# Preparing q, k and v between the input units, and running half of the attention heads inside the last seven of them

## The reference, cut to what matters

```python
h = rms_norm(x, g_mix)                                   # 1024 tokens x 1024
q_down, kv_down, k_rope, conv_in, gate_logits = split(h @ w_in)
q  = rms_norm(q_down) @ w_uq;   kv = rms_norm(kv_down) @ w_ukv      # 8 heads
k_nope, v = split(kv);          k = concat(k_nope, k_rope)
q, k = rope(rms_norm(q)), rope(rms_norm(k))              # norm per head, 96 wide
y_a = softmax(q @ k.T * scale, chunk-causal mask) @ v @ w_o
u = c_val * sigmoid(c_gate)
u = silu(layer_norm(causal_depthwise_conv(u, 31 taps) + b_dw))
y_b = u @ w_conv_out
x = x + (sigmoid(gA) * y_a + sigmoid(gB) * y_b) @ w_out
x = x + moe(rms_norm(x))                                 # 4 groups x 8 experts, top 2
```

## Time and profile before

| | us |
|---|---|
| median of 3 runs | 1285.98 (1282.86 to 1286.04) |
| the profiled execution, its own time | 1280.47 |
| its span, first to last instruction | 1278.4 |
| PE busy in the span | 1178.3 (92%) |
| DVE, ACT, POOL busy | 751.0 (59%), 469.2 (37%), 198.9 (16%) |
| mean granted clock of PE | 0.955 |
| PE busy and granted clock from 60 to 350 us (input units) | 288.93 of 290, 1.00 |
| from 350 to 460 us (attention, tiles 0 to 3) | 92.04 of 110, 0.88 |
| from 460 to 620 us (attention, tiles 4 to 7) | 153.48 of 160, 0.97 |
| from 620 to 710 us (branches) | 89.31 of 90, 0.98 |

### The profile page before, as it was taken

The page is one execution under the profiler, slowest core; times in us unless marked ns, Lnnn a source line. Parts: engine busy times, 40 slices in busy tenths (PEclk is TensorE's granted clock), DMA queues, the critical chain, the costliest instruction groups (busy, mean ns, idle before and its releaser), DMA issues.

```text
span 1278.4 us, 14988 instructions
## 1 busy us (share of the span) xinstructions
PE 1178.3 (92%) x5452; PEld 896.4 (70%) x5452; DVE 751.0 (59%) x992; ACT 469.2 (37%) x635; POOL 198.9 (16%) x243
## 2 busy tenths in 40 slices
PE   5999999999968999999899899849999988989996
PEld 5988888887645667767788788746676665666664
DVE  3338999993424455444466434476776656656663
ACT  4432111113443444444232211124555544554552
POOL 4010000000142232220000000011222321222211
PEclk8999999999969999999799999958999999999999
DMA  6011111110100000001330233495999999999980
GB/s 224 1 50 50 49 49 49 49 49 17 42 0 1 1 1 1 1 1 34 131 83 17 90 113 129 169 320 179 324 339 320 304 322 316 334 333 314 308 267 8
DMA packets 101542, 172.28 MB, mean 135 GB/s; under 512 B 11727, under 2 KB 45690, under 8 KB 101498
## 3 DMA queue, kind: packets, MB, share of 16 engines
q1 hardware_dynamic: 91002, 154.86, 35.8%
q0 software_dynamic: 10432, 16.81, 5.4%
q10 hardware_dynamic: 64, 0.02, 0.0%
HBM read 165.35 MB, written 27.26 MB: 151 GB/s over the span
## 4 chain that ended last, share of the span: by engine, by line
PE 71%; DMA 12%; ACT 4%; DVE 4%; issue 4%; POOL 2%; SPq 2%; DVEq 0%; ACTq 0%; POOLq 0%
PE pb L1224 15%; PE pb L1226 15%; PE pb L1225 15%; DMA wgu_raw<-in_w_e_up 11%; PE pb L1506 7%; PE pb L1364 4%; PE pb L1341 4%; PE pb L1353 2%; PE pb L1273 2%; PE pb L1478 2%; PE pb L1283 1%; PE pb L1424 1%; ACT wgu_hi L772 1%; SPq L414 1%; SPq L418 1%
## 5 line engine op out<-in xcount | busy, mean ns | idle before, releaser
L1165 DVE TENSOR_TENSOR wgu_lo<-wgu_raw,wgu_hi 128x2048 fp32r<-128x2048 f32 x72 | 164.7, 2289 | 89.3 <-ACT wgu_hi L772 87.8
L1506 PE MATMUL pb<-wed,midT 128*128 128x512 f32 x288 | 136.5, 618 | 23.1 <-DVE midT L1200 23.0
L873 DVE SCALAR_TENSOR_TENSOR cv<-up,dwc,cv 128x1024 f32<-128x1024 f32 x120 | 154.1, 1284 | 3.7
L1224 PE MATMUL pb<-hT_hi,ws_hi 128*128 128x512 f32 x384 | 151.7, 395 | 0.0
L772 ACT ACTIVATE wgu_hi<-wgu_raw 128x2048 fp32r<-128x2048 f32 x72 | 137.1, 1909 | 38.0 <-DMA wgu_raw<-in_w_e_up 33.8
L1226 PE MATMUL pb<-hT_hi,ws_lo 128*128 128x512 f32 x384 | 149.5, 389 | 0.0
L1225 PE MATMUL pb<-hT_lo,ws_hi 128*128 128x512 f32 x384 | 149.5, 389 | 0.0
L1224 PE MATMUL pb<-wgu_hi,hgT_hi 128*128 128x512 f32 x288 | 130.0, 452 | 0.0
L1506 PEld LDWEIGHTS pb<-wed,midT 128*128 128x128 f32 x288 | 54.6, 196 | 87.2 <-issue 62.5
L1226 PE MATMUL pb<-wgu_hi,hgT_lo 128*128 128x512 f32 x288 | 113.2, 393 | 0.0
L1225 PE MATMUL pb<-wgu_lo,hgT_hi 128*128 128x512 f32 x288 | 112.5, 391 | 0.0
(11 more groups left out here) (281 smaller groups left out, 2019.9 us busy)
## 6 DMA issues: line engine op xcount, KB each, us to landing
wgu_raw<-in_w_e_gate SPq DMA_DIRECT2D x36, 1024.0 KB
wgu_raw<-in_w_e_up SPq DMA_DIRECT2D x36, 1024.0 KB
wed<-in_w_e_down SPq DMA_DIRECT2D x36, 1024.0 KB, 16.3
ws_raw<-in_w_in SPq DMA_DIRECT2D x24, 512.0 KB, 3.9
xs<-in_x SPq DMA_DIRECT2D x8, 512.0 KB, 8.4
wout<-in_w_out SPq DMA_DIRECT2D x1, 4096.0 KB, 12.9
xb<-in_x SPq DMA_DIRECT2D x8, 512.0 KB, 5.2
h_rows<-h SPq DMA_DIRECT2D x8, 512.0 KB, 2.7
```

Source lines behind the costliest of these rows:

```text
L873: i = v.scalar_tensor_tensor(out=cv[:, c, :], in0=src, scalar=w, in1=cv[:, c, :], op0=ALU.mult, op1=ALU.add)
L1165: v.tensor_tensor(wgu_lo[q % SLOTS][:, :, ks, :], wgu_raw[q % SLOTS][:, :, ks, :], wgu_hi[q % 2][:, :, ks, :].bitcast(F32), ALU.subtract). ...
L1224: t_.matmul(out, w(0), m(0), start=start, stop=False)
L1506: m = t_.matmul(pb[:, 4 + h, :], midT[:, f, :], wed[q][:, f, h * 512:(h + 1) * 512], start=(f == 0), stop=(f == 1))
```

## The change

- **Preparation** (`prep`, the nine pieces of a tile in the order `PREP`) moves between the k-slices of the input units: 16 steps to a unit, tile t in units 1+2t and 2+2t, at the steps of `PREP_STEP`. Two PSUM banks (6 and 7) take turns. ACT copies `qdT` and writes the squares back into PSUM; DVE sums them `SUMS_LATE` = 4 steps and scales kT `K_LATE` = 2 steps after PE's step. The finished q, k, v of a tile go to DRAM and are loaded back later, as the space in SBUF is taken.
- **Heads 0 to 31** (tiles 0 to 3) run between the k-slices from unit 17, step 8, one head to three steps: `probs_T(n)` and `scores(n+2)` at one step, `pv(n)` two steps later. Tiles 4 to 7 follow the units as before, without preparation between the heads.
- **The gates** go to DRAM from a buffer of two (`gst`) and come back after attention, 16 transfers of 512 KB.
- **Taps**: 6 to a unit in place of 7, spread over the steps of a unit.
- **Layer norm** moves to tiles 4 to 6: POOL adds the four channel groups (six additions of 1024 columns), PE does four matmuls in place of 16, ACT and DVE do their parts between heads (`MEAN_AT` to `CONV_SPLIT`).
- **The split of the attention output** is made per tile from PSUM (`attn_hi`, `attn_lo`), `attn_T` of tiles 0 to 3 in heads 33 to 36, of tile 7 inside the first branch unit.

```diff
-TAPS_PER_UNIT = 7
+TAPS_PER_UNIT = 6
+STEPS = 2 * KD
+MIXED = 4 * 8
...
+        PREP = ("qdT", "q0", "q1", "kv0", "kv1", "qT0", "qT1", "kT0", "kT1")
+        PREP_STEP = (0, 3, 6, 9, 12, 22, 24, 28, 30)
+        PREP_UNIT = 1
+        SUMS_LATE, K_LATE = 4, 2
...
+        HEAD0, PER_HEAD = STEPS * 17 + 8, 3
+        attn_T_at = {MIXED + 1: 0, MIXED + 2: 1, MIXED + 3: 2, MIXED + 4: 3, 42: 4, 50: 5, 58: 6}
+        MEAN_AT, SQUARE_AT, VAR_AT, SQRT_AT = (37, 38), (39, 40), (44, 45), 46
+        RECIP_AT, SCALE_AT, SILU_AT, CONV_SPLIT = (47, 48, 49, 50), (51, 52), 53, (55, 56)
+        def prep_slot(kind, t):
+            n = len(PREP) * t + PREP.index(kind)
+            return n % 2, n // 2 + 1
...
+            sp.wait_ge(pv_ok, NTILE * HEADS)
+            for b in range(2):
+                sp.wait_ge(gate_out[b], 16 * GATE_UNITS // 2)
+            load_gates(0)
+            load_gates(1)
+            sp.wait_ge(cv_lo, NC)
+            sp.dma_start(wout[:, :, :], w_out[0].rearrange("(k p) c -> p k c", p=P)).then_inc(wout_in, 16)
...
@@ ACT: the loop over the input units
                 if u + 2 < IN_UNITS:
                     unit_hi(u + 2)
+                for s in range(STEPS):
+                    g = STEPS * (u + 1) + s
+                    if g in prep_at:
+                        prep(*prep_at[g])
+                    if g - 2 in scores_at:
+                        exps(scores_at[g - 2])
...
@@ DVE: before the loop over the input units
+            rotary_angles()
+            link(v.tensor_scalar(ss3[:, 2, :], ss3[:, 2, :], 1.0 / QK, EPS, ALU.mult, ALU.add))
@@ DVE: the loop over the input units
                 if u + 2 < IN_UNITS:
                     unit_lo(u + 2)
+                fresh = max(0, target - taps_done)
+                for s in range(STEPS):
+                    for k in range(taps_done + fresh * s // STEPS, taps_done + fresh * (s + 1) // STEPS):
+                        tap(k)
+                    g = STEPS * (u + 1) + s
+                    if prep_at.get(g - SUMS_LATE, ("",))[0] in ("q0", "q1", "kv0", "kv1"):
+                        prep(*prep_at[g - SUMS_LATE])
+                    if prep_at.get(g - K_LATE, ("",))[0] in ("kT0", "kT1"):
+                        prep(*prep_at[g - K_LATE])
+                    if g - 1 in probs_at:
+                        probs_out(probs_at[g - 1])
+                    if g - 1 in scores_at:
+                        rowmax(scores_at[g - 1])
...
@@ PE
+            def prep(kind, t):
+                b, count = prep_slot(kind, t)
+                if count > 1:
+                    pe.wait_ge(prep_free[b], count - 1)
...
+            def attn_T(t):
+                pe.wait_ge(on_ok, t + 1)
+                if t:
+                    pe.wait_ge(at_lo, t)
...
+            def unit(u):
+                b = u % 2
+                for f in range(2):
+                    for k in range(KD):
+                        g = STEPS * u + f * KD + k
+                        if g in prep_at:
+                            prep(*prep_at[g])
+                        if g in probs_at:
+                            probs_T(probs_at[g])
+                        if g in scores_at:
+                            scores(scores_at[g])
+                        if g in pv_at:
+                            pv(pv_at[g])
+                        i = three(pb[:, 2 * b + 2 + f, :], lambda s: ws[s][:, b, k, :], lambda s: hT[s][:, k, f * 512:(f + 1) * 512], k == 0, k == KD - 1)
```

More of the change, by code:

```diff
@@ L154, in build @@
     ONO = room(2 * K)
-    On = place("On", [P, HEADS * VD], F32, ONO)
     QDO = room(NTILE * DOWN * 4)
+    On = [place(f"On{i}", [P, HEADS * VD], F32, QDO + 2 * K * i) for i in range(4)]
     qd = place("qd", [P, NTILE, DOWN], F32, QDO)
@@ L384, in _, with unit_col, prep_freed, store_prep @@
-            sp.wait_ge(u_hi, IN_UNITS)
-            sp.wait_ge(u_lo, IN_UNITS)
+            def unit_col(u):
+                if u < GLU_UNITS:
+                    return (VALUE_COL if u % 2 else GATE_COL) + (u // 2) * P
+                return LOGIT_COL + (u - GLU_UNITS) * P
+            def prep_freed(*pieces):
+                for piece in pieces:
+                    b, count = prep_slot(*piece)
+                    sp.wait_ge(prep_free[b], count)
+            def store_prep(u):
+                t, late = divmod(u - PREP_UNIT, 2)
+                if not 0 <= t < NTILE:
+                    return
+                if late:
+                    prep_freed(("qT0", t), ("qT1", t))
+                    sp.dma_start(qT_d[t], qst[0:QK, :]).then_inc(q_out, 16)
+                    prep_freed(("kT0", t), ("kT1", t))
+                    sp.dma_start(kT_d[t], kst[0:QK, :]).then_inc(k_out, 16)
+                else:
+                    prep_freed(("kv0", t), ("kv1", t))
+                    sp.dma_start(v_d[t], vst[:, :]).then_inc(v_out, 16)
@@ L651, in _ @@
             down_out(NTILE - 1)
+            act.wait_ge(sin_in, 1)
+            a.activation(sincos[:, :, :, :], sincos[:, :, :, :], ACT.Sin).then_inc(sin_ok, 1)
             for u in range(IN_UNITS):
@@ L1034, in wout_rest @@
+            attn_lo(NTILE - 1)
             def wout_rest(k, count):
@@ L1270, in misc @@
                     pe.wait_ge(uq_in, 16)
+                    if kind == "q0":
+                        bb, cc = prep_slot("qdT", t)
+                        pe.wait_ge(prep_free[bb], cc)
                     c0 = 4 * QK * (kind == "q1")
@@ L1384, in _ @@
-            misc("oT", NTILE - 1)
-            pe.wait_ge(m_free, len(order))
-            def branches(b, first=False):
-                for br_ in (1, 0):
-                    for f in range(2):
-                        for k in range(4):
-                            if first and f == 0 and k % 2 == 0:
-                                pe.wait_ge(sp_lo, 1 + k // 2 + 2 * (1 - br_))
-                            i = three(pb[:, 4 * b + 2 * br_ + f, :], lambda s: ws[s][:, b, 4 * br_ + k, :],
-                                      lambda s: aT[s][:, 4 * br_ + k, f * 512:(f + 1) * 512], k == 0, k == 3)
-                i.then_inc(u_mm, 1)
@@ L1398, in _, with branch @@
-            for b in range(2):
-                pe.wait_ge(u_lo, IN_UNITS + b + 1)
-                branches(b, b == 0)
+                if n in attn_T_at:
+                    attn_T(attn_T_at[n])
+                if n in MEAN_AT:
+                    ln_mean(MEAN_AT.index(n))
+                if n in VAR_AT:
+                    ln_square(VAR_AT.index(n))
+                pv(n)
+            def branch(b, br_):
+                for f in range(2):
+                    for k in range(4):
+                        i = three(pb[:, 4 * b + 2 * br_ + f, :], lambda s: ws[s][:, b, 4 * br_ + k, :],
+                                  lambda s: aT[s][:, 4 * br_ + k, f * 512:(f + 1) * 512], k == 0, k == 3)
+                return i
@@ L1401, in _ @@
+            pe.wait_ge(u_lo, IN_UNITS + 1)
+            pe.wait_ge(cv_lo, NC)
+            branch(0, 1)
+            attn_T(NTILE - 1)
+            pe.wait_ge(at_lo, NTILE)
+            branch(0, 0).then_inc(u_mm, 1)
+            pe.wait_ge(u_lo, IN_UNITS + 2)
+            branch(1, 1)
+            branch(1, 0).then_inc(u_mm, 1)
             with pe.Fori(1, OUT_UNITS // 2) as i:
@@ L1404, in _ @@
                     pe.wait_ge(yab_used, i * 2 + (b - 1))
-                    branches(b)
+                    branch(b, 1)
+                    branch(b, 0).then_inc(u_mm, 1)
             pe.wait_ge(wo_lo_ok, 6)
```

613 lines of the change are left out of this document (327 added, 286 removed).

## The result

The changed kernel takes 1.0254 times as long as the kernel before, 95% interval 1.0221 to 1.0287. Four executions took 1313.5, 1321.4, 1334.5 and 1339.2 us (the ratio rests on the first two, since the comparison leaves out an execution over 1.5% above the kernel's fastest), against 1282.9 to 1286.0 before. The prediction of 1291 had the sign right and the size wrong, and its range ended at 1308. The profiled execution took 1313.5, 33 us more than the one before.

A forecast was written before the change was run, and what follows sets the result against it. PE was taken as the bound: 495.5 us of work plus (a) to (f) gave 556.0 against 550.3; with the branch units' gain of 0.5, +5 on 1286 made 1291 us. Own range 1283 to 1298; two in ten outside 1266 to 1308.

The forecast's parts named there:

- (f): Half clock on PE after the waits of 4.4, 3.2 and 4.7 us, 1.7 each: 5.1 us, bounds 0 and 17.
- all 44 us of waits and half clock of before: PE's stretch of 550.3 us less 506 of work; waits and half clock that the change can take.
- (a): First tile: PE at q0 waits for ACT's qdT, which stands behind the sine and a sigmoid: 4.4 us.
- (e): Tiles 4 to 7: waits for attention low parts, layer norm, Silu, splits and the step into the tail: 18.8 us.
- cost PE the same wherever they stand: Units, preparation, heads and transposes keep their PE cost when moved; with layer norm shrunk, work is 495.5 us.
- (b): q0 of tiles 1 to 7 waits for DVE's kT copy behind unit_lo: 1.8 us seven times, 12.6.
- (c): kT0 of each tile waits for POOL's k chain, held by taps: 8 us, the middle of 0 and 15.6.
- (d): Mixed units 18 to 22: the first pv waits for DVE's copy of pT behind the low part: 11.6 us.
- the 140 to 160 I had set: Range in us for the tail of 32 heads; outside it the prediction would count as wrong.
- Branches and experts: Stages after attention: length to stay unchanged, with the branch units gaining 0.5 us.
- The gates' way through DRAM: After attention, 16 transfers of 512 KB, 23 us in all, hidden under 87 us of branch matmuls: cost nothing.
- Rival B: POOL's chain waits for three taps (15.6 us), six or more waits drop the clock (12): 1306 us, chance 20%.

The follow-up runs named there:

- the undone version with two waits: The fastest version with the attention's low part behind the row maximum again in heads 34 and 35 only: ratio 0.9772.
- without taps: The changed kernel with 29 of the 31 taps of each channel block of the convolution left out: ratio 1.0252.
- the fastest version: Changed kernel with earlier k copy, sums and qd copies, reordered low parts, later pv, whole pT of heads 54 and 55 on DVE: 1247.1 us, ratio 0.9715.
- the unmixed heads: Changed kernel with six edits (1264.2 us together), then heads of tiles 0 to 3 moved behind the last input unit: ratio 1.0173.

## Why the prediction was wrong

**The step that failed is (f), the clock**: 5.1 us, bounds 0 and 17; it was 20 in the profiled execution. It went wrong in three places. I took the shortest gap with a row, 3.5 us, for what it takes and counted only waits over 2 or 3 us; the clock fell behind one of 1.94 us in unit 18 and behind those of 1.6 us in tile 4. I took 3.4 us of half clock for each fall; it was 3.4 to 10.2 us in one piece here, 13.7 in the undone version with two waits and 41 without taps. And all 44 us of waits and half clock of before were struck out, also those at the end of tile 7, which the change does not touch (6.5 us of half clock there after it).

Two of the three stood in the trace of the kernel before. There PE idles for 1.69 us at 371.6 and for 2.30 at 607.1, and 1.9 and 1.3 us behind their ends begin 13.7 us of half clock each (at 375.2 and at 610.7); I had read only the gap of 3.5. The columns are as in the table of stages:

```profile
370.00:375.00 5.00, 3.11 (x13) 1.77 (x13) 1.35 (x3) 2.53 (x8) 2.73 (x3) 1.00 0.00 0
375.00:380.00 5.00, 3.67 (x19) 2.90 (x19) 2.09 (x7) 2.26 (x9) 4.60 (x7) 0.52 0.00 0
...
606.00:610.00 4.00, 1.70 (x16) 1.46 (x15) 1.83 (x2) 3.74 (x5) 0.00 (x0) 1.00 0.00 0
610.00:614.00 4.00, 3.54 (x21) 3.13 (x20) 0.43 (x1) 0.43 (x1) 0.00 (x0) 0.59 0.00 0
614.00:618.00 4.00, 3.67 (x16) 3.49 (x16) 2.58 (x3) 1.97 (x2) 0.00 (x0) 0.50 0.00 0
```

The clock is also what the four executions differ by. Their spans of 1311.6, 1319.6, 1332.7 and 1337.4 us have mean granted clocks of 0.955, 0.950, 0.939 and 0.935. The span times what is missing to 1 gives 59, 66, 81 and 87 us lost: 7, 22 and 28 more than in the first, where the times are 8, 21 and 26 longer. So (f) was further off in the executions that were not profiled.

**The sum again, by what was measured.** PE was busy for 525.5 us of the 578.1: 52.6 idle, where (a) to (e) gave 55.4 (-2.8); 20.3 lost to half clock (half of the 40.6), where (f) gave 5.1 (+15.2); the other 505.2 is work, where 495.5 was forecast (+9.7). Together 556.0 + 22.1 = 578.1.

- *Work.* Low by 9.7, the second miss. The step that failed is "cost PE the same wherever they stand". In the fastest version, free of half clock, the same stretch has 503.3 us of PE work, 7.8 above the forecast: 1.8 in units 0 to 16, 8.3 in units 17 to 23 (2.6 of them the two scores), and 2.4 less in the tail. The other 1.9 of the changed kernel I can't place. The price of a head itself was about right: the estimate from the unmixed heads is 51 us for 32, with the two scores in it. Among unit matmuls a head costs some 0.2 us more. What it is, is not settled; that it is not the number of breaks is shown.
- *(a), (b), (c), (d)* were right in place and size, and each was removed by taking away what it named (behind (b) stood a wait of 0.6 for ACT, seven times). In (c) the size is luck: I took the middle between 0 and 15.6 for want of a reason. The hold was 0.94 to 0.98 us for each of three instructions, where 1.3 was the bound. With it the chain ends at 7.6 + 2.9 = 10.5 and PE is there at 9.1, which is the wait of 1.4 that three of the four tiles beside gate units have (the fourth has 2.1, three of the others 0.6).
- *(e)* was right for the sum of its waits (18.8 forecast; 17.9 measured, with the 4.3 for DVE's pT and 1.2 of issue) and for its two large ones (6.4 for 6.4, 4.4 for 4.7); the small ones do not match one by one (3.8 us for DVE's pT in tile 7, where 1.4 stood for the weight splits). It was wrong in that they cost no clock. The tail took 156.7 us, inside the 140 to 160 I had set.
- *Branches and experts.* The gates' way through DRAM cost nothing: the branches' 1.9 more is the last tile's split, 1.4, and the eighth set of transposes. I had them gain 0.5, since the half clock in their first unit was struck out too; it reaches 3.7 us into that unit before and after. The 2.4 behind them is less than this part differs by among the variants (570 to 576, against 568.8 before).
- *Rival B* had the right kind of miss, six or more waits that drop the clock, and still gave 1306, 8 us of it for a (c) of 15.6 that did not come (8.2). It needed the longer stretches as well.

The change itself is sound in what it moves: mixing saves 48 us against the same heads alone in the profiled executions. Its 2.5% came from program order on DVE and ACT, where low parts, a maximum and a high part stood ahead of the small operations that PE was waiting for.

## What to carry to other kernels

A short wait on the bounding engine has two prices, its length and the clock that it can cost; the second has no fixed size and was the larger one here in tile 4 without taps (28 us in all for 6.4 of waits), so look at the granted clock behind every gap, not only behind the long ones. Read the kernel before in this way too, ahead of a forecast. Where executions of one kernel scatter, compare their mean granted clocks, and stage by stage where there are profiles: here the stages whose length differed while their instructions and waits did not were stages at half clock. And in a program written in order, put behind the small operation that PE waits for whatever is not needed before the next unit; here such edits took the kernel from 1.0254 to 0.9715 of the one before.
